# Latent attention in a two-block transformer kernel: the softmax weights' scaling moves from VectorE to ScalarE

## The reference, cut to what matters

```
s = jnp.einsum('bhqd,bhkd->bhqk', q_blk, k).astype(jnp.float32)
s = jnp.where(k_pos[None, :] <= q_pos[:, None], s, NEG_INF_2)
p = jax.nn.softmax(s, axis=-1).astype(v.dtype)
return jnp.einsum('bhqk,bhkd->bhqd', p, v)
```

## Time and profile before

| | |
|---|---|
| median of 3 runs | 2246.6 us (2246.54 to 2250.92) |
| the profiled execution | 2245.73 us, of which the trace's span is 2243.4 us |
| PE busy | 2199.0 us, 98% of the span |
| PE weight loads busy | 1886.2 us, 84% |
| DVE busy | 1616.6 us, 72% |
| ACT busy | 1125.0 us, 50% |
| mean granted TensorE clock | 0.994 of full speed |
| the latent attention | from about 1367 to 1404 us |

### The profile page before, as it was taken

One profiled execution on the slowest core, in us unless ns is written; L12 is line 12 of the kernel. 1 busy time (PEld: TensorE's weight loads), 2 busy tenths in 40 slices (PEclk: granted clock), 3 DMA queues, 4 the chain that ended last, 5 costly groups with the idle time before them and its releaser, 6 DMA issues.

```text
span 2243.4 us, 30610 instructions
## 1 busy us (share of the span) xinstructions
PE 2199.0 (98%) x12162; PEld 1886.2 (84%) x12162; DVE 1616.6 (72%) x2447; ACT 1125.0 (50%) x1691; POOL 24.5 (1%) x58
## 2 busy tenths in 40 slices
PE   7999999999999999999999999989999999999998
PEld 7999887888888888888879886878888888888987
DVE  6998885899998799998865666566555555544455
ACT  5434774555554455554454656545444444444443
POOL 1000000000000000000000000000000000000000
PEclk9999999999999999999999999999999999999999
DMA  8644435688889888889945551547666667655553
GB/s 272 214 166 140 154 95 206 225 291 285 293 307 369 313 280 292 289 287 353 334 154 180 178 173 47 198 135 245 230 227 224 226 229 232 216 190 190 184 187 121
DMA packets 137694, 500.97 MB, mean 223 GB/s; under 512 B 15472, under 2 KB 15616, under 8 KB 137040
## 3 DMA queue, kind: packets, MB, share of 16 engines
q1 hardware_dynamic: 136512, 494.43, 65.2%
q0 software_dynamic: 752, 2.49, 0.6%
q10 hardware_dynamic: 288, 2.10, 0.2%
HBM read 496.47 MB, written 2.49 MB: 222 GB/s over the span
## 4 chain that ended last, share of the span: by engine, by line
PE 84%; DVE 12%; ACT 3%; issue 1%; DMA 0%; POOL 0%; SPq 0%; DVEq 0%; ACTq 0%; POOLq 0%
PE bank L601 19%; PE both L601 18%; PE bank L604 10%; PE both L604 9%; PE bank L591 8%; DVE w_lo L1640 5%; PE bank L592 4%; PE bank L594 4%; PE bank L596 4%; PE bank L595 4%; DVE raw L1622 2%; ACT ffn_a L1364 1%; ACT ffn_g L1370 1%; PE bank L841 1%; PE both L798 1%
## 5 line engine op out<-in xcount | busy, mean ns | idle before, releaser
L1640 DVE TENSOR_TENSOR w_lo<-raw,w_hi 128x1024 fp32r<-128x1024 f32 x737 | 894.2, 1221 | 458.5 <-ACT w_hi L1166 456.8
L1166 ACT ACTIVATE w_hi<-raw 128x1024 fp32r<-128x1024 f32 x737 | 768.4, 1054 | 647.2 <-PE bank L604 296.1
L591 PE MATMUL bank<-h_both,w_hi 128*128 128x512 f32 x1408 | 357.3, 395 | 1.3 <-DVE h_both L1694 1.3
L591 PEld LDWEIGHTS bank<-h_both,w_hi 128*128 128x128 f32 x1408 | 253.5, 190 | 46.2 <-DVE h_both L1694 1.8
L1622 DVE SCALAR_TENSOR_TENSOR raw<-raw,silu_c 128x1024 f32<-128x1024 f32 x192 | 233.9, 1218 | 0.0
L601 PE MATMUL bank<-w_hi,h_both 128*128 128x512 f32 (+2 forms) x1024 | 233.8, 372 | 0.0
L601 PE MATMUL both<-w_hi,h_both 128*128 128x512 f32 (+1 forms) x960 | 231.9, 383 | 1.1 <-DVE h_both L1714 1.1
L601 PEld LDWEIGHTS bank<-w_hi,h_both 128*128 128x128 f32 x1024 | 181.8, 188 | 33.0 <-ACT w_hi L1166 0.3
L592 PEld LDWEIGHTS bank<-h_both,w_lo 128*128 128x128 f32 x1408 | 192.7, 191 | 13.8
L601 PEld LDWEIGHTS both<-w_hi,h_both 128*128 128x128 f32 x960 | 171.4, 191 | 33.5 <-DVE h_both L1714 2.0
L592 PE MATMUL bank<-h_both,w_lo 128*128 128x256 f32 x1408 | 196.8, 283 | 0.0
(11 more groups left out here) (357 smaller groups left out, 2634.9 us busy)
## 6 DMA issues: line engine op xcount, KB each, us to landing
raw<-weights SPq DMA_DIRECT2D x924, 512.0 KB, 4.5
raw<-weights SPq DMA_DIRECT2D x5, 504.0 KB, 3.5
x<-x SPq DMA_DIRECT2D x2, 1024.0 KB, 5.8
bias<-bias_rows POOLq DMA_DIRECT2D x8, 256.0 KB, 10.6
silu_c<-c ACTq DMA_DIRECT2D x2, 1024.0 KB, 4.7
out<-x SPq DMA_DIRECT2D x8, 256.0 KB, 2.1
phase<-params SPq DMA_DIRECT2D x1, 497.0 KB, 10.6
raw<-weights SPq DMA_DIRECT2D x1, 488.0 KB, 3.7
```

The lines of the kernel that those rows point to most:

```text
L591: return e.matmul(out, hi, a_both[:, k, :, :].rearrange("p a t -> p (a t)"), start=first, stop=last)
L1166: e.activation(w_hi[:, n % PART_SLOTS, 0:widths[i]], raw[:, i % RAW_SLOTS, 0:widths[i]], ACT.Copy).then_inc(hi_ready, 1)
L1640: e.tensor_tensor(w_lo[:, slot, 0:widths[i]], raw[:, i % RAW_SLOTS, 0:widths[i]], w_hi[:, slot, 0:widths[i]].bitcast(F32), ALU.subtract).t ...
```

## The change

Only the latent attention of the second block is touched. VectorE keeps the reciprocal and signals it on a new semaphore `m_inverted`. The multiplication becomes a ScalarE copy in place with the per-row factor as its scale, placed in ScalarE's turn u behind `latent_exp(u)` for unit u-1. `m_weighted`, for which TensorE's transposes wait, now comes from ScalarE.

```diff
-        m_scored, m_taken, m_maxed, m_exped, m_weighted = sem("m_scored"), ...
+        m_inverted, m_scored, m_taken, m_maxed, m_exped, m_weighted = sem("m_inverted"), ...
@@ scalar_program
+            def latent_weights(u):
+                s = m_scores[:, u % 3, 0:P * (m_units[u][1] + 1)]
+                w.wait_ge(m_inverted, u + 1)
+                e.activation(s, s, ACT.Copy, scale=m_sum[:, u:u + 1]).then_inc(m_weighted, 1)
+
             def latent_transpose(u):
@@ scalar_program, the loop over u
                 next(linear, None)
                 if u < NM:
                     latent_exp(u)
+                if 1 <= u < NM + 1:
+                    latent_weights(u - 1)
@@ vector_program
             def latent_weights(u):
-                s = m_scores[:, u % 3, 0:P * (m_units[u][1] + 1)]
                 w.wait_ge(m_exped, u + 1)
-                t = chain(e.reciprocal(m_sum[:, u:u + 1], m_sum[:, u:u + 1]))
-                w.wait_ge(dve_step, t)
-                e.tensor_scalar(s, s, m_sum[:, u:u + 1], None, ALU.mult).then_inc(m_weighted, 1)
+                e.reciprocal(m_sum[:, u:u + 1], m_sum[:, u:u + 1]).then_inc(m_inverted, 1)
```

More of the change, by code:

```diff
@@ L519, in two_blocks @@
         k_nope_ready, mla_v_ready = sem("k_nope_ready"), sem("mla_v_ready")
-        m_scored, m_taken, m_maxed, m_exped, m_weighted = sem("m_scored"), sem("m_taken"), sem("m_maxed"), sem("m_exped"), sem("m_weighted")
+        m_inverted, m_scored, m_taken, m_maxed, m_exped, m_weighted = sem("m_inverted"), sem("m_scored"), sem("m_taken"), sem("m_maxed"), sem("m_exped"), sem("m_weighted")
         ff_turned = sem("ff_turned")
```

## The result

The changed kernel is slower by about a quarter of a percent: 2251.57 us, the median of 9 runs (2251.1 to 2254.48), against 2245.68 us for the kernel before, also the median of 9 runs (2244.76 to 2250.92; the three known at the time of the prediction, with 2246.6 as their median, are among them). The ratio is 1.0027, with a 95% interval of 1.0019 to 1.0035: 4.3 to 7.9 us more. The profiled execution took 2251.21 us, with a span of 2248.9 us against 2243.4.

The account below looks back on a forecast made before the run. The prediction took TensorE's order of work as the bound overall, VectorE in the loop's first pairs. Six pairs' 6.4 us plus 1.1 at the start gave 7.5 us, so 2254.1 us, range 2250.0 to 2259.0.

Parts of the forecast that it names:

- The forecast's own bounds: Whole change: 5.7 to 9.6 us added, 2252.3 to 2256.2 us on the median, before widening for noise.
- The lower bound, 5.7: Whole change: 5.7 us added if all 16 copies take the bare copy's 0.28 and 0.38 us.
- What bounds the kernel: TensorE's order of work overall; VectorE from 1377.93 to 1391.50; the loop's loss is handed on to the end in full.
- The copies' price: ScalarE's 16 scaling copies take 0.39 us for 128 columns and 0.50 for 256, with no table load added.
- The place in the queue: Scaling copy behind ScalarE's exp closes a ring with TensorE's transpose; 7.5 us, against 2.0 by durations alone.
- The two-tile turn: Loop turn that transposes two tiles: 2.22 us with GLA steps, 1.86 without.
- the one-tile turn: Loop turn that transposes one tile: 2.47 us with GLA steps, 2.05 without.
- The start and the end: First transpose 0.54 us later, unit 2's 1.1 later; the last copy, hidden under an output projection piece, costs nothing.
- VectorE's relief: Rival, 1377.94 to 1391.50: relieving VectorE makes the kernel faster by 1 us, at the very most 2.6; chance 0.03.
- the ring: Each loop turn: scaling copy, transpose, output product, `mix_hi`, GLA step, exp, next copy; six pairs add 6.4 us.
- Only the durations count: Rival: ScalarE's slack takes the copies and TensorE loosens the ring; 2.0 us more, 2248.6 us; chance 0.11.
- The clock in the loop: Rival: TensorE's clock falls to 1.2 GHz in the sparser loop, some 10 us in six pairs, 2266 us; chance 0.06.

Follow-up runs that it names:

- the GpSimd kernel: On the kernel before, GpSimd inverts the row sums and VectorE only multiplies; 2243.12 us, ratio 0.9986.
- the kernel with the extra copies outside the ring: The kernel before plus 16 ScalarE copies behind each turn's exp, into a tile nobody reads, VectorE still scaling the weights; 2245.6 us, ratio 0.9995.
- the kernel with the extra copies in the ring: The changed kernel plus the same 16 unread ScalarE copies, between the exp and the copy that scales the weights; 2258.86 us, ratio 1.0057.

## Why the prediction came out right, step by step

The time was forecast at 2254.1 us with a range of 2250.0 to 2259.0, and 0.83 on slower by over 0.2%. It is 2251.57, and the ratio of 1.0027 is on the forecast side of 1.002, though its interval (1.0019 to 1.0035) just reaches that bound. The mechanism came out as told; the size was 1.6 us too large (7.5 against 5.9), and the other 0.9 of the 2.5 us between 2254.1 and 2251.57 is the kernel before, whose median fell from 2246.6 to 2245.68 with more runs. Some luck is in the range. The forecast's own bounds were 2252.3 to 2256.2, and the median lies below them; it is in the range because that was widened for noise. The lower bound, 5.7, was priced by copies of 0.28 and 0.38 us, and the copies took 0.39 and 0.50: what made the result small was something else, which the range did not price.

*What bounds the kernel:* right in the main. VectorE was in the way in the first pairs, but the GpSimd kernel gained only half of what a bound by VectorE alone would have given, so something else stood close behind it. The 6.1 us at 1494.99 to 1501.10 had gone undiminished through TensorE's full stretch; what I had not seen is that 0.64 of it would come back in the clock's low stretch.

*The copies' price:* taken as 0.39 and 0.50, measured 0.392 and 0.496. No table load was added.

*The place in the queue:* right as the mechanism. The extra copies cost nothing in one place and their full time from start to start in the other, and turning two instructions round on ScalarE takes back 5.2 of 5.9 us of the loop. The two-tile turn was calculated at 2.22 and is 2.22.

*The term that was mis-sized:* the one-tile turn, 2.47 expected and 2.34 measured, six times in the six pairs. The link is the one from the transpose to `mix_hi`. I took 0.95 from the earlier trace rows, and it is 0.81 (1378.64 to 1379.45): the output product starts 0.17 instead of 0.20 behind the transpose and is 0.61 instead of 0.71 long. Its weight loads (PEld L1084) start together with the transpose now; before, they started together with the product, 0.2 us later. It isn't the longer idle time of TensorE that does this. Before, a transpose that TensorE had waited 0.92 us for has the late loads too, and in the kernel with the copy ahead of the exp a wait of 0.41 us is enough for the early ones (the first three rows are of the kernel before, the fourth is of the changed kernel, the last three are of the kernel with the copy first):

```profile
1397.79 0.33 PE L1074 MATMUL bank<-lasting,m_scores 128*128 128x128 f32 x1 [0.92 <-DVE m_scores L2259]
1397.98 0.52 PEld L1084 LDWEIGHTS bank<-m_T,mla_v 128*128 128x128 f32 x4
1397.98 0.71 PE L1084 MATMUL bank<-m_T,mla_v 128*128 128x128 f32 x4
...
1378.64 0.58 PEld L1084 LDWEIGHTS bank<-m_T,mla_v 128*128 128x128 f32 x4
...
1381.54 0.33 PE L1074 MATMUL bank<-lasting,m_scores 128*128 128x128 f32 x1 [0.41 <-ACT m_scores L1523]
1381.54 0.58 PEld L1084 LDWEIGHTS bank<-m_T,mla_v 128*128 128x128 f32 x4
1381.70 0.61 PE L1084 MATMUL bank<-m_T,mla_v 128*128 128x128 f32 x4
```

What goes with it is the engine that wrote the transposed weights: in the traces with the product behind the transpose, the loads come late for every one-tile unit from unit 2 on that VectorE scaled, and early for every one that ScalarE scaled. Why is open. So a row read where VectorE released the transpose was carried over into a ring where ScalarE does. Six times 0.13 make 0.78 of the 0.8 us by which the six pairs came out shorter (5.56 against 6.4); without the GLA steps the turn is 1.92 instead of 2.05, the same 0.13.

*The start and the end:* the first transpose is 0.53 later (0.54 expected), unit 2's 0.98 (1.1 expected). The end costs nothing, as expected, and gains 0.12.

*The sum:* 7.5 expected, 6.4 from the table load to the last transpose, 5.5 in the two profiled spans, 5.9 by the medians. Of the 2.0 us between 7.5 and the spans, 1.1 is the mis-sized turn with the start and the end, 0.28 lies ahead of the table load and 0.64 behind the loop.

*The rivals:* VectorE's relief gives nothing back as long as the copy is in the ring (true, and the GpSimd kernel shows that a smaller relief pays where no ring takes its place). Relieving the busiest engine of the stretch made the loop 5.9 us longer here. One argument against that rival was wrong: 10.78 and 4 x 0.89 us of copies were said to be more than ScalarE has in 13.57 us, but the kernel with the extra copies outside the ring does both in 13.57 us, with ScalarE busy 12.64. "Only the durations count" gave 2.0 us, and the kernel with the copy ahead of the exp, where it comes nearest to holding, has 0.7. The clock in the loop stayed at 1.00 in the changed kernel, and fell in part in the kernel with the extra copies in the ring, so this rival may have been nearer than 0.06 made it look.

## What to carry to other kernels

Before moving a step to an engine with free time, follow the result round: who waits for it, and does the receiving engine itself wait for them in its next turn. If so, nearly the step's full length is added to every turn, however idle the engine is; here the same copy was free outside the ring and 0.3 to 0.4 us a turn inside it. Put such a step ahead of the receiving engine's other work of that turn, or give the small, early half of it (here the reciprocal) to an engine that stands outside.

## What the runs showed of the hardware

The granted clock, which I had seen fall in this kernel only round the norms, also fell inside a loop without long gaps, where TensorE did short products between waits for ScalarE (0.78 of full speed on average from 1404 to 1408 us in the kernel with the extra copies in the ring, a mixture of 2.4 and 1.2 GHz). The pair of turns concerned took 0.77 us more. The TensorE product behind a one-tile transpose started sooner and was shorter where ScalarE had written the tile than where VectorE had, 0.17 and 0.61 us against 0.20 and 0.71, whatever TensorE's idle time before it. GpSimd's power on a 128 x 1 column took 0.55 us, which made it a usable place for reciprocals that are due a turn later. ScalarE started an ACTIVATE 0.09 us before the scaling copy ahead of it had ended (0.29 us apart for a length of 0.39, from 1381.09 to 1381.38 in the kernel with the copy first). Behind an exp with a read of its accumulator there was no such gain: 0.49 us apart for 0.50 (1382.27 to 1382.76 in the changed kernel).
